# Expert results scaled at eviction and added into the residual by accumulating gathers in two passes

## The chip, the cores and the metric

The kernel is written in Bass, engine by engine, for one core of a Trainium2 chip. The metric is the device time of one execution in microseconds; lower is better.

## What is computed

A decoder trunk of two layers on 1024 tokens of width 1024, in float32. Each layer is an RMSNorm, one input projection shared by four kinds of heads, an output projection, a residual add, an RMSNorm and a mixture of experts, again with a residual add. The kernel ends with a norm. Only the end of the mixture of experts matters here:

```python
e_w = jax.nn.softmax(e_top, axis=-1) * g_p            # weights of a token's two experts
...
def expert_block(args):
    xb, e = args
    return (jax.nn.silu(xb @ w_gate[e]) * (xb @ w_up[e])) @ w_down[e]

ys = lax.map(expert_block, (xs, block_e)).reshape(n_slots, d)
return jax.ops.segment_sum(ys * slot_w[:, None].astype(ys.dtype), slot_tok, num_segments=t)
```

There are 32 experts with 256 hidden columns; each token goes to 2 of them, so 2048 rows are computed per layer, 64 per expert on average.

## The kernel before

**Data.** `X` (`residual`) holds the residual in SBUF: 128 partitions x 8 tiles of 128 tokens x 1024. `HT` (`normed_cols`) holds normed rows turned into columns, `YT` (`heads_cols`) the heads' results, `WR` (`w_ring`) weights. During the expert stage `WR` and `HT` hold gate and up weights of four experts (`Wgu`), `YT` their down weights (`Wd`), and most else lies in `G` (`group_arena`). In DRAM, `h2_dram` (`h_rows`) has the normed rows of all tokens and `ys_dram` (`expert_rows`) the experts' results, by slot: a slot is a row of a block of 128 rows, and there are 39 blocks and one more.

**Units.** VectorE ranks the experts by how many rows they have and gives every assignment of a token a slot (`dest_i`, two per token). The 16 experts with most rows are singles, with a block each; the other 16 go in pairs, 64 rows of a block for each. A block is a unit, so there are 24, ordered in eight "quads" of three: single, single, pair. Rows over an expert's share go to overflow units behind them, in a loop that a counter read from SBUF ends. Blocks 0 to 15 are the singles, 16 to 23 the pairs; quad q has the singles 2q and 2q + 1 and the pair 16 + q.

**The unit.** GpSimd gathers its rows of `h2_dram` into `xg` (an indirect DMA, line 747). TensorE turns them (L1238, L1244), ScalarE and VectorE take a half each (L1679, L2336), TensorE multiplies with gate and up (`gate_up`, L1259), ScalarE takes the silu (L1683), VectorE multiplies (L2340), TensorE turns (L1267), VectorE takes that (L2344), TensorE multiplies with down (`down`, L1280), and ScalarE and VectorE copy a half of the result each into `yb` (`take_y`, L1688, L2349). SyncE stores it to `ys_dram` (`store_y`, L645). TensorE's program is staggered: unit u's `gate_up`, then the turns of unit u - 1's hidden rows and of unit u + 1's inputs, then unit u - 1's `down`. VectorE and ScalarE follow in that order. Weights are loaded by SyncE in its program order: gate and up of the next quad (L620, L621) behind the end of this quad's `gate_up`, down (L624) behind the end of `down`. GpSimd issues all 24 row gathers, each as soon as its buffer is free.

**Start of the stage.** Behind the slot indices (`idx_i`, L2315) VectorE works out the overflow counter and the tokens' weights `wts` (L2318 to L2332), then takes its half of the first unit's rows. TensorE runs matmuls without use until the first rows are there (L1214).

**End of the stage.** SyncE, ScalarE, VectorE and TensorE pass the overflow loop; TensorE, ScalarE and VectorE meet in a barrier. GpSimd waits for all stores and issues 16 gathers of 512 KB, two per tile, from `ys_dram` into buffers `back`:

```python
for k in range(2):
    pool.indirect_dma_start(
        out=back[t][k], out_offset=None, in_=ys_dram,
        in_offset=bass.IndirectOffsetOnAxis(ap=dest_i[:, k, t:t + 1], axis=0)
    ).then_inc(back_in[t], 16)
```

VectorE combines tile by tile (`combine`, L2385): X += back0 * w0, X += back1 * w1. Then follows the norm of a tile: ScalarE squares and sums (L1359), VectorE scales the sum (L1777), ScalarE takes the root (L1361), VectorE inverts it (L1780) and writes the normed rows (L1781). TensorE turns them (L791, `turn_normed`), and ScalarE alone copies both halves (`take_whole_tile`, L1353). VectorE combines tile t + 1 before it norms tile t. At the kernel's start the norm of x has the same form without a combine, and there ScalarE and VectorE take a turned half each (`take_tile`: L1353, L1770).

**Into the next layer.** In layer 0 TensorE computes the next layer's first products behind the turns: behind tile 4's turn the first, which uses tiles 0 to 3, and one more behind each of tiles 5, 6 and 7 (`next_use`, L805). Their weights, chunks 0 and 1 of the input projection (1 MB and 2 MB), are loaded by SyncE into `WR` (`load_first`, L534) when all results are stored. In the last layer there is no product; SyncE stores each normed tile to the output (L683).

## Time and profile before

| | us |
|---|---|
| median of 3 runs | 2563.99 |
| lowest and highest | 2562.85, 2568.65 |
| the profiled execution | 2559.61 |
| its span (first to last instruction) | 2557.8 |
| TensorE busy | 2312.9 (90%) |
| VectorE busy | 1205.5 (47%) |
| ScalarE busy | 896.1 (35%) |
| GpSimd busy | 176.9 (7%) |

All times of rows are microseconds from the start of the span. Busy shares are means over stages with different limits: TensorE's 90% says little of the tails behind the two expert stages, of some 40 us each, where it mostly waits. The granted clock of TensorE is 1.00 at its full level, 2.4 GHz, and 0.50 at the lower, 1.2 GHz. "To landing" is the time from a DMA's issue to its semaphore. A gather's row names the tile that it fills: `group_arena` or `heads_cols` for the results, since `back` lies there.

### The profile page before, as it was taken

How to read it: one execution, taken by the hardware profiler on the slowest of the kernel's cores; microseconds unless marked ns; L12 is line 12 of the kernel's file. 1: busy time of each engine (PE TensorE's matmuls, PEld its weight loads, DVE VectorE, ACT ScalarE, POOL GpSimd, SP SyncE). 2: the span in 40 equal slices, each digit the busy share in tenths (PEclk: the TensorE clock that was granted, in tenths of full speed). 3: DMA queues.
4: the chain of work that ended last, by engine and by line, in shares of the span. 5: the costliest groups of instructions: out<-in, count | busy, mean ns of one | idle time of the engine just before them, and what ended most of it. 6: DMA issues, size and time to landing. Idle time of an engine off the chain costs nothing.

```text
span 2557.8 us, 29586 instructions
## 1 busy us (share of the span) xinstructions
PE 2312.9 (90%) x10142; PEld 1285.4 (50%) x10142; DVE 1205.5 (47%) x2666; ACT 896.1 (35%) x1842; POOL 176.9 (7%) x355
## 2 busy tenths in 40 slices
PE   5999989788999999999589998997989999899993
PEld 3476434555665554444246654445656655444442
DVE  4435288876663341111333445788766623311115
ACT  2122278864552111111222313797645511111113
POOL 0000032000000000000200000410000000000002
PEclk9999999899999989999799999998999999899996
DMA  6110001220100059999710001014010010799995
GB/s 255 28 52 27 33 14 43 80 63 1 50 1 28 33 216 371 422 423 422 297 43 30 33 27 37 14 52 129 2 50 1 1 36 33 302 408 422 422 414 214
DMA packets 101106, 353.79 MB, mean 138 GB/s; under 512 B 20246, under 2 KB 39660, under 8 KB 76396
## 3 DMA queue, kind: packets, MB, share of 16 engines
q1 hardware_dynamic: 89456, 310.15, 31.2%
q0 software_dynamic: 11520, 41.95, 4.3%
q8 instruction: 77, 1.26, 0.2%
q14 instruction: 53, 0.43, 0.1%
HBM read 296.03 MB, written 55.91 MB: 138 GB/s over the span
## 4 chain that ended last, share of the span: by engine, by line
PE 62%; DVE 13%; issue 8%; DMA 8%; ACT 6%; POOL 1%; SPq 1%; PEldq 1%; PEld 1%; DVEq 0%; ACTq 0%; POOLq 0%
PE bank L802 10%; PE bank L1259 9%; PE bank L1152 9%; DMA w_ring<-in_expert_w_up 7%; PE bank L882 6%; PE bank L791 6%; PE bank L805 5%; PE bank L1280 4%; PE bank L914 4%; ACT group_arena L1540 3%; DVE group_arena L2006 2%; DVE residual L2385 1%; PE bank L1169 1%; PE bank L1214 1%; DVE group_arena L1781 1%
## 5 line engine op out<-in xcount | busy, mean ns | idle before, releaser
L802 PE MATMUL bank<-w_ring,normed_cols 128*128 128x260 f32 (+4 forms) x1280 | 436.9, 494 | 10.7 <-ACT heads_cols L1565 8.9
L802 PEld LDWEIGHTS bank<-w_ring,normed_cols 128*128 128x128 f32 x1280 | 239.4, 193 | 180.1 <-issue 153.4
L805 PE MATMUL bank<-normed_cols,w_ring 128*128 128x512 f32 x640 | 281.1, 599 | 7.1 <-ACT group_arena L1442 6.2
L791 PE MATMUL bank<-ident,group_arena 128*128 128x128 f32 (+1 forms) x1200 | 183.4, 295 | 113.6 <-DVE group_arena L1781 91.2
L1259 PE MATMUL bank<-w_ring,group_arena 128*128 128x512 f32 x512 | 227.5, 597 | 7.5 <-DMA w_ring<-in_expert_w_up 4.0
L1152 PE MATMUL bank<-w_ring,heads_cols 128*128 128x512 f32 x512 | 225.5, 595 | 2.0 <-DVEq L261 2.0
L791 PEld LDWEIGHTS bank<-ident,group_arena 128*128 128x128 f32 (+1 forms) x1200 | 146.7, 150 | 158.3 <-issue 80.4
L805 PEld LDWEIGHTS bank<-normed_cols,w_ring 128*128 128x128 f32 x640 | 122.0, 193 | 158.7 <-issue 150.8
L882 PE MATMUL bank<-group_arena 96*128 96x512 f32 (+7 forms) x384 | 155.8, 510 | 25.1 <-ACTq L1430 13.1
L1280 PE MATMUL bank<-heads_cols,group_arena 128*64 128x512 f32 (+1 forms) x512 | 173.8, 596 | 2.8 <-DVE group_arena L2344 2.8
L2344 DVE COPY group_arena<-bank 128x256 f32<-128x256 f32 x48 | 20.3, 424 | 320.9 <-PE bank L1267 320.9
L1856 DVE TENSOR_REDUCE softmax_stats<-bank 128x1 f32<-128x768 f32 (+6 forms) x144 | 136.2, 946 | 62.1 <-PE bank L887 42.9
L1259 PEld LDWEIGHTS bank<-w_ring,group_arena 128*128 128x128 f32 x512 | 95.3, 190 | 135.9 <-issue 123.2
L1152 PEld LDWEIGHTS bank<-w_ring,heads_cols 128*128 128x128 f32 x512 | 95.3, 191 | 111.2 <-issue 108.9
L1540 ACT ACTIVATE group_arena<-heads_cols,group_arena 128x896 bf16<-128x896 f32 (+1 forms) x124 | 135.8, 1095 | 35.8 <-DVEq L2068 21.3
L2026 DVE TENSOR_SCALAR_CACHE_REDUCE group_arena<-group_arena 128x512 bf16<-128x512 f32 (+3 forms) x200 | 141.6, 754 | 11.5 <-DVE group_arena L2067 10.3
L747 POOL DMA_INDIRECT group_arena<-h_rows,group_arena x48 | 45.4, 945 | 1376.1 <-DVEq L2316 935.4
L1683 ACT ACTIVATE group_arena<-bank 128x256 f32<-128x256 f32 x48 | 18.4, 383 | 325.8 <-PE bank L1259 325.8
L1259 PE MATMUL bank<-normed_cols,group_arena 128*64 128x512 f32 x512 | 113.4, 595 | 11.1 <-DMA normed_cols<-in_expert_w_up 11.1
L1353 ACT ACTIVATE group_arena<-bank 128x512 f32<-128x512 f32 (+1 forms) x108 | 63.6, 589 | 141.7 <-PE bank L791 140.7
L2006 DVE SCALAR_TENSOR_TENSOR group_arena<-heads_cols,group_arena 128x512 f32<-128x512 f32 (+3 forms) x140 | 92.2, 658 | 25.3 <-ACT heads_cols L1531 18.6
L1770 DVE COPY group_arena<-bank 128x512 f32<-128x512 f32 (+4 forms) x124 | 69.3, 559 | 71.1 <-PE bank L791 68.6
(351 smaller groups left out, 3024.7 us busy)
## 6 DMA issues: line engine op xcount, KB each, us to landing
heads_cols<-in_expert_w_down SPq DMA_DIRECT2D x64, 1024.0 KB, 13.3
w_ring<-in_expert_w_gate SPq DMA_DIRECT2D x32, 1024.0 KB, 17.0
w_ring<-in_expert_w_up SPq DMA_DIRECT2D x32, 1024.0 KB, 19.1
normed_cols<-in_expert_w_gate SPq DMA_DIRECT2D x32, 1024.0 KB, 14.7
normed_cols<-in_expert_w_up SPq DMA_DIRECT2D x32, 1024.0 KB, 16.7
expert_rows<-group_arena SPq DMA_DIRECT2D x48, 512.0 KB, 13.5
w_ring<-in_w_in SPq DMA_DIRECT2D x6, 2048.0 KB, 9.0
expert_rows<-heads_cols SPq DMA_DIRECT2D x1, 8192.0 KB, 27.7
```

What stands on the lines that cost most here:

```text
L791: last = pe.transpose(bank(4 + r % 2)[0:rows, col:col + src.shape[0]], src, ident[0:src.shape[0], 0:src.shape[0]])
L802: m = pe.matmul(out[:, 0:width], HT[:, k, part * P:(part + 1) * P], w, start=(k == 0), stop=(k == K - 1))
L805: m = pe.matmul(out[0:width, :], w, HT[:, k, part * HALF:(part + 1) * HALF], start=(k == 0), stop=(k == K - 1))
L882: m = pe.matmul(L[:, c0:c1], a["q"](h, t), a["k"](h, c0, c1), start=True, stop=not (by_choice or diagonal))
L914: pe.matmul(O[i * HD:(i + 1) * HD, pair * P:(pair + 1) * P], KINDS[kind]["v"](h, b), pT[:, u % 2, at:at + P], start=(b == 0), stop=(b == t))
L1152: m = pe.matmul(bank(n % 4)[:, :], YT[:, k, t * P:(t + 1) * P], WR[:, (OUT_CHUNK + c) % 2, k, :], start=(k == 0), stop=(k == K - 1))
L1259: m = pe.matmul(gu_bank(s)[rows, :], xgT[:, s, k, rows], Wgu[w][:, :, k, :], start=(k == 0), stop=(k == K - 1))
L1280: m = pe.matmul(bank(6 + h)[rows, :], aT[:, s, k, rows], Wd[w][:, k, h * HALF:(h + 1) * HALF], start=(k == 0), stop=(k == 1))
L1540: act.activation(sign_junk[:, 0:w], flipped[t], ACT.Sign, bias=trial_bias[:, t - 2:t - 1], scale=SIGN_SCALE, accum_out=thr[:, 0, t - 2:t - ...
L1856: dve.tensor_reduce(stats(tile, heads[0], m, 1), src, AX_X, ALU.max, negate=True).then_inc(max_ready, 1)
L2006: ins = dve.scalar_tensor_tensor(s, rel[:, i, at:at + w], wI[:, t, j:j + 1], s, ALU.mult, ALU.add)
L2026: chain.go(dve.tensor_scalar(to, src(t), limit(t), 0.0, ALU.is_ge, ALU.add, accum_out=thr[:, 0, t - 2:t - 1]))
```

## The change

**Weights at eviction.** The two copies of a unit's result now multiply each row by its slot's weight: `take_y` gets `scale`, a column of `slot_w` (128 rows x 40 blocks). `slot_w` is made in unit 0: VectorE splits `wts` into three bfloat16 parts that add up to it, and builds masks; TensorE sums their products in 16 matmuls of 120 columns (`weights_to_slots`) between unit 1's turns and unit 1's `gate_up`; VectorE adds the parts (`spread_weights`). VectorE's `take_x(0, 0)` stands ahead of all this. The quad loops of ScalarE and VectorE are unrolled, since the weight's column differs by unit.

**Results added by DMA.** `back`, `combine` and `back_used` are gone. GpSimd gathers rows of `ys_dram` straight into `X` with addition, in two passes of 16. In the first the indices of late slots (blocks 14, 15, and 23 and up) are raised by 2^20, past the bound, so that their rows are skipped; in the second all others are. The first pass begins when the units of quad 6 are stored and all weights have landed; the second when all units are stored. Every gather waits until the one before it on the same tile has landed.

**Order elsewhere.** `load_first` of chunk c now comes ahead of the last three stores, behind the `gate_up` of units 21 and 22; overflow units use weight buffer 2 instead of 0. At the start, two more regions of `ys_dram` are zeroed (3 more blocks). Behind the barrier ScalarE waits for `back_in[t]` and squares; VectorE and ScalarE take a turned half each.

```diff
+        TURN_ORDER = [(0, 0), (1, 0), (2, 0)] + [at for t in range(T) for at in ((t, 1), (t + 3, 0)) if at[0] < T]
...
             sp.wait_ge(setup_zero, 1)
-            sp.dma_start(ys_dram[UNITS * P:, :].rearrange("(a p) d -> p a d", p=P),
-                         YT[:, 0:1, :].to_broadcast([P, SLOT_ROWS - UNITS, D])).then_inc(setup_dma2, 16)
+            for a, b in ((SINGLES - QUAD_SINGLES, SINGLES), (UNITS - 1, SLOT_ROWS)):
+                sp.dma_start(ys_dram[a * P:b * P, :].rearrange("(a p) d -> p a d", p=P),
+                             YT[:, 0:1, :].to_broadcast([P, b - a, D])).then_inc(setup_dma2, 16)
...
+                for c in range(2):
+                    sp.wait_ge(gu_done, UNITS - QUAD_UNITS + c + 1)
+                    with sp.If(l < DEPTH - 1):
+                        load_first(nc.s_assert_within(l + 1, 1, DEPTH - 1,
...
                 for i in range(QUAD_UNITS):
                     store_y(UNITS - QUAD_UNITS + i, unit_block(QUADS - 1, i), i)
...
+                def add_rows(t, k, at_i, n):
+
+                    wait_later(pool, back_in[t], 16 * n)
+                    pool.indirect_dma_start(
+                        out=X[:, t, :], out_offset=None, in_=ys_dram,
+                        in_offset=bass.IndirectOffsetOnAxis(ap=at_i[:, k, t:t + 1], axis=0),
+                        bounds_check=SLOT_ROWS * P - 1, oob_is_err=False, compute_op=ALU.add).then_inc(back_in[t], 16)
+
                 pool.wait_ge(idx_ready, 2)
+                for s in range(QUAD_UNITS):
+                    pool.wait_ge(y_out[s], 16 * (QUADS - 1))
+                for w in range(NW):
+                    pool.wait_ge(dn_in[w], 16 * QUADS)
+                for t, k in TURN_ORDER:
+                    add_rows(t, k, early_i, k)
+                pool.wait_ge(slot_weights, 1)
...
                 for s in range(QUAD_UNITS):
                     pool.wait_ge(y_out[s], 16 * QUADS)
+                for t, k in TURN_ORDER:
+                    add_rows(t, k, late_i, 2 + k)
                 for t in range(T):
...
-                    pool.wait_ge(back_in[t], 32)
+                    pool.wait_ge(back_in[t], 64)
...
-                    act.activation(yb[:, s, 0:HALF], bank(6), ACT.Copy).then_inc(y_lo, 1)
+                    act.activation(yb[:, s, 0:HALF], bank(6), ACT.Copy, scale=scale).then_inc(y_lo, 1)
...
-                        act.wait_ge(back_used, t + 1)
+                        act.wait_ge(back_in[t], 64)
                         norm_tile(t, T + t + 1)
                     if t >= 1:
-                        take_whole_tile(t - 1)
+                        take_tile(t - 1)
...
+                chain(dve.tensor_copy(w_parts[:, 0, :, :], wts[:, :, :]))
+                chain(dve.tensor_tensor(w_rest, wts[:, :, :], w_parts[:, 0, :, :], ALU.subtract))
+                chain(dve.tensor_copy(w_parts[:, 1, :, :], w_rest))
+                chain(dve.tensor_tensor(w_parts[:, 2, :, :], w_rest, w_parts[:, 1, :, :], ALU.subtract))
+                for k in range(2):
+                    chain(dve.tensor_tensor(blk_one, blk_of_slot, slot_at[:, 1:2, k * T:(k + 1) * T].to_broadcast([P, SLOT_ROWS, T]),
+                                            ALU.is_equal))
+                    chain(dve.tensor_tensor(w_hot[:, k, :, :, :], blk_one.unsqueeze(1).to_broadcast([P, 3, SLOT_ROWS, T]),
+                                            w_parts[:, :, k, :].unsqueeze(2).to_broadcast([P, 3, SLOT_ROWS, T]), ALU.mult))
+                chain(dve.tensor_copy(row_hot_w, row_hot))
+                dve.sem_inc(v2p, 1)
...
-                    dve.tensor_copy(yb[:, s, HALF:], bank(7)).then_inc(y_hi, 1)
+                    dve.tensor_scalar(yb[:, s, HALF:], bank(7), scale, None, ALU.mult).then_inc(y_hi, 1)
...
-                combine(0)
-                for t in range(T):
-                    if t + 1 < T:
-                        combine(t + 1)
-                    norm_tile(t, 4 * T + t + 1, T + t + 1)
+                for t in range(T + 1):
+                    if t < T:
+                        norm_tile(t, 4 * T + t + 1, T + t + 1)
+                    if t >= 1:
+                        take_tile(t - 1)
```

The order of a pass, as (tile, which of its two gathers), is (0,0) (1,0) (2,0) (0,1) (3,0) (1,1) (4,0) (2,1) (5,0) (3,1) (6,0) (4,1) (7,0) (5,1) (6,1) (7,1). The eight small operations that make the two index tables (`early_i`, `late_i`) stand on VectorE behind the copy of `row_hot_w`, ahead of unit 0's product.

## Rows read from the trace of the kernel before

**Rows 1.** The page: GB/s that the DMA engines moved, in 40 equal slices.
```profile
GB/s 255 28 52 27 33 14 43 80 63 1 50 1 28 33 216 371 422 423 422 297 43 30 33 27 37 14 52 129 2 50 1 1 36 33 302 408 422 422 414 214
```

**Rows 2.** Windows: us, then busy us and instructions by engine, TensorE's clock, DMA share, GB/s.
```profile
45.00:60.00 15.00, 15.00 (x48) 7.56 (x47) 2.73 (x5) 1.95 (x5) 0.00 (x0) 1.00 0.00 1
970.00:975.00 5.00, 5.00 (x21) 2.87 (x20) 1.44 (x3) 0.98 (x2) 0.94 (x1) 1.00 0.39 129
1230.00:1235.00 5.00, 5.00 (x26) 1.73 (x24) 0.43 (x1) 0.34 (x1) 0.00 (x0) 1.00 0.75 308
1235.00:1240.00 5.00, 4.48 (x17) 1.74 (x13) 0.75 (x2) 0.38 (x1) 0.00 (x0) 1.00 0.01 5
1265.00:1270.00 5.00, 1.94 (x8) 1.57 (x8) 4.46 (x6) 1.61 (x6) 4.09 (x4) 0.50 1.03 399
2490.00:2495.00 5.00, 5.00 (x26) 1.58 (x22) 0.00 (x0) 0.00 (x0) 0.00 (x0) 1.00 0.54 220
```

**Rows 3.** The chain of waits, layer 0: start us, us, what.
```profile
1246.95 2.62 DMA expert_rows<-group_arena
```

**Rows 4.** The timeline, layer 0's last unit and tail: start us, us, engine, line, operation.
```profile
1246.19 0.69 DVE L2349 COPY group_arena<-bank 128x512 f32<-128x512 f32 x1 [3.76 <-PE bank L1280]
...
1250.41 0.94 POOL L769 DMA_INDIRECT group_arena<-expert_rows,group_arena  x1 [60.23 <-DMA expert_rows<-group_arena]
1251.65 0.94 POOL L769 DMA_INDIRECT heads_cols<-expert_rows,group_arena  x1 [0.30 <-issue]
...
1256.87 1.28 DVE L2385 SCALAR_TENSOR_TENSOR residual<-group_arena,residual 128x1024 f32<-128x1024 f32 x1 [9.99 <-DMA heads_cols<-expert_rows,group_arena]
...
1284.25 1.97 PE L791 MATMUL bank<-ident,group_arena 128*128 128x128 f32 x8 [2.66 <-DVE group_arena L1781]
```

**Rows 5.** The timeline, last layer's tail.
```profile
2515.55 1.28 DVE L2385 SCALAR_TENSOR_TENSOR residual<-group_arena,residual 128x1024 f32<-128x1024 f32 x1 [10.05 <-DMA heads_cols<-expert_rows,group_arena]
...
2552.80 1.28 DVE L1781 SCALAR_TENSOR_TENSOR group_arena<-residual,rstd,gain 128x1024 f32<-128x1024 f32 x1
```

**Rows 6.** The gathers of results (line 769): ns min/median/max; landing from issue.
```profile
L769 POOL DMA_INDIRECT group_arena<-expert_rows,group_arena x16: 933/938/1906, 1250.4 to 2529.6; - x16
...
DMA to landing us min/median/max: 4.2/7.5/12.9
```

**Rows 7.** The timeline, start of the kernel: first norms of x.
```profile
16.53 1.06 ACT L1359 ACTIVATE group_arena<-residual 128x1024 f32<-128x1024 f32 x1
...
31.67 1.28 DVE L1781 SCALAR_TENSOR_TENSOR group_arena<-residual,rstd,gain 128x1024 f32<-128x1024 f32 x1
...
33.70 1.94 PE L791 MATMUL bank<-ident,group_arena 128*128 128x128 f32 x8 [1.76 <-DVE normed_cols L1770]
...
38.09 1.28 DVE L1781 SCALAR_TENSOR_TENSOR group_arena<-residual,rstd,gain 128x1024 f32<-128x1024 f32 x1
```

**Rows 8.** The timeline, start of layer 0's expert stage.
```profile
942.73 0.69 DVE L2311 TENSOR_TENSOR group_arena<-group_arena 128x1024 f16<-128x1024 f16 x1
...
943.54 0.83 PE L1230 MATMUL bank<-group_arena 128*128 128x40 f16 x8 [1.19 <-DVEq L2313]
...
946.29 0.15 DVE L2318 TENSOR_SCALAR group_arena<-group_arena 128x1 f32<-128x1 f32 x1
...
949.51 0.17 DVE L2332 TENSOR_TENSOR group_arena<-group_arena 128x8 f32<-128x8 f32 x1
...
954.58 0.69 DVE L2336 COPY group_arena<-bank 128x512 f32<-128x512 f32 x1 [4.90 <-PE bank L1244]
...
964.18 7.10 PE L1259 MATMUL bank<-w_ring,group_arena 128*128 128x512 f32 x16 [0.83 <-ACT group_arena L1679]
```

**Rows 9.** DMA issues of the whole kernel: KB each, median us to landing.
```profile
expert_rows<-heads_cols SPq DMA_DIRECT2D x1, 8192.0 KB, 27.7
...
normed_cols<-forgetting_q_k SPq DMA_DIRECT2D x2, 2048.0 KB, 19.9
```

153 lines of the change are left out of this document (87 added, 66 removed).

## The prediction

> **What bounds the kernel now.** I read the views from the whole to the place. The page's row of DMA rates [rows 1] shows the two expert stages as the stretches near 420 GB/s. The windows [rows 2] then say when the transfers stop: the rate is full until 75% of the window 1230 to 1235, so until 1233.7 us, and the next window moves nothing. TensorE still has 12.5 us of its last units: its last result is evicted at 1246.19 [rows 4]. In the last layer the transfers stop at 2492.7 (54% of 2490 to 2495, rows 2). So behind each expert stage there is a hole of 12 us in the DMA engines, and it is there that the change puts work. After the last eviction comes the tail: the store of the last unit (2.62 us [rows 3]), GpSimd's first gather 0.84 us behind its landing, and VectorE's first combine at 1256.87 [rows 4]. From there VectorE sets the pace: two combines of 1.28 us and a norm per tile, 4.63 us a tile. What the tail is worth differs by layer. In layer 0, TensorE needs tile 4 before its first product of the next layer (turned at 1284.25 [rows 4]); from there its own products set the end. So only tile 4 counts, 27.4 us behind the first combine. In the last layer tile 7 counts: normed at 2554.08, 38.5 us behind the first combine at 2515.55 [rows 5], with only its store behind it.
>
> **What is removed.** 16 combines per layer, 32 x 1.28 = 41 us of VectorE work. The rest of a tile then has the form of the kernel's start: ScalarE squares, VectorE norms and both engines take the turned halves, which is what the new loops do. The start shows the pace [rows 7]: first square at 16.53, norms at 31.67 (tile 4) and 38.09 (tile 6), so 3.2 us a tile. From "tile 0 complete" to "tile 4 turned" it takes 33.70 - 16.53 = 17.2 us; to the end of the eighth norm 38.09 + 2.7 + 1.28 - 16.53 = 25.6 us, with the one table load and TensorE at its lower clock, as in the tail (granted clock 0.50, rows 2). Against the 27.4 and 38.5 us of today this gives back **10.2 us in layer 0 and 12.9 us in the last layer**, if tile 0 is complete at the time of today's first combine.
>
> **What is added, and when tile 0 is complete.** GpSimd now issues 16 accumulating gathers, then 16 more, in one fixed order. No tile is complete before the second pass reaches it, and the second pass begins only when the first is issued. An issue takes 0.94 us and 0.30 between [rows 4, 6], so the first pass takes at least 16 x 1.24 = 19.8 us, and it starts only when all weights have landed: 1233.7 + 0.8 (GpSimd's wake) + 1.6 (below) = 1236.1, and 2495.1. (7,1), the last of the first pass, waits for (7,0), the 13th.
>
> The unknown is the DMA time of one accumulating gather; no row shows one. The lower end is a plain copy: 512 KB at 420 GB/s [rows 1], 1.25 us. A gain below that has no reason. The upper end is the slowest large transfer, 2048 KB in 19.9 us [rows 9], or 5.0 us per 512 KB. I take 2.5 us: it is nearest to the plain row, but an addition needs two operands, the row from memory and the old residual, and I price the second read like the first. About a tenth of the rows is left to the second pass (my estimate: of 2048 rows over 32 experts, the two singles and the pair that are late hold near the mean of 64, the pair less), so 2.25 us. The Trainium skill ("Collectives: The Full Stack", section on the bandwidth ceiling) says that an addition in a DMA emits two read descriptors per chunk on one ring and that reduce-scatter therefore runs at half of all-gather, 32.35 against 62.28 GB/s; no row here shows it. By that rule the sum stays as below, and by the plain row alone it is the first rival.
>
> Landing of the 13th, last layer: 2495.1 + 0.94 + 13 x 2.25 + two stores in between (2.5) + 2.0 (what a landing takes beyond issue and transfer: 4.2 - 0.94 - 1.25 [rows 6]) = 2529.8. The last three land 6.75 later, at 2536.6. The second pass moves little, but stands behind them: (0,0) at about 2536.8, (0,1) waits for it and lands 3.2 later: tile 0 is complete at 2540.0. The last norm ends 25.6 later, at 2565.6: **+11.5 us** against 2554.1.
>
> Layer 0 has the same and two things more in the queue: the store of unit 21 (1.25) and the next layer's first weights, which the change moves ahead of the last stores: 3 MB, 7.5 us at 420 GB/s. SyncE's queue is not held by that wait: the unit that it waits for is done before the store behind it can be issued. But the transfer fills the hole. So the 13th lands at 1236.1 + 0.94 + 29.25 + 2.5 + 8.75 + 2.0 = 1279.5, the last at 1286.3, tile 0 is complete at 1289.7, tile 4 is turned at 1306.9: **+22.6 us** against 1284.25. Moving the load gains nothing: those 7.5 us end today long before tile 4 is turned at 1284.25.
>
> **The start of the expert stage.** VectorE's weight work moves behind its first copy of turned rows, which ends at 955.27 [rows 8]. Moved: the 3.4 us from 946.29 to 949.68. New: four small operations (0.8), the masks (two of 320 and two of 960 elements; 1024 two-byte elements take 0.69: 2.1), a copy of 2048 (1.35), eight small ones (1.6). End 964.5; with the product (0.41) and the next copy (0.69) behind it the second unit's matmuls start at 965.75 instead of 964.18 [rows 8]: **+1.6 us a layer**, already in the sums. Bounds -0.6 (faster copies; nothing gained below the 0.83 us that TensorE waits now) and +2.8 (masks at four-byte pace). It isn't absorbed: TensorE is the bound there, and the DMA share falls to 0.39 in 970 to 975 [rows 2], so the loads shift too. The 16 small matmuls are covered by that wait (8 take 0.83 [rows 8]); without it they would cost 1.7.
>
> **Costed at nothing.** The scale in the evictions: one operation takes another's place, 0.69 us [rows 4], hidden by TensorE but for the last unit's. The 1.5 MB more of zeros at the start: the first fill takes 27.7 us [rows 9] and the DMA engines are idle from 45 to 60 [rows 2]; uncovered it would be 3.7 us. The unrolled loops: no engine but TensorE is near its limit there. The last store under load: it lands before the first pass has been issued. Overflow units don't run: the first gather of the tail waits for nothing but the last store [rows 4].
>
> Sum: 22.6 + 11.5 = 34.1 us. The profiled execution took 2559.6 us (span 2557.8), 4.4 under the median of 2564.0, against which I set the forecast: **2598 us**.
>
> **Rivals.**
> 1. *The addition is free, 1.25 us a gather (1.12 with a tenth missing).* For it: TensorE's hole is filled, and memory reads are what the copy rate measures. Against: the second operand. With the queue as above the 13th lands at 2515.1 and 1264.9, and tile 0 is complete at 2523.3 and 1273.0: -5.2 and +6.0, about 2565, no change. If the next layer's weights don't stand in the way (they may have landed by then), GpSimd's pace alone decides: the second pass starts at 1255.9 and 2514.9, tile 0 is complete 6.9 later, -4.2 and -6.7: 2553, **faster**. The mechanism decides at tile 0 complete by 1267 and 2528; that is at a gather of about 1.4 us. Chance 0.35, of it 0.24 for faster, 0.11 for no change.
> 2. *Skipped rows cost as much as moved ones* (the passes don't do what they say). Both passes then move 16 x 2.5 us. Last layer: tile 7 is complete 40 us behind 2540.6, and its norm ends at 2583.7, +29.6; layer 0: tile 4 is complete at 1320.3, turned at 1324, +40. About 2634. Against: the skipped index is outside the table. Chance 0.06.
> 3. *The addition runs at the slow row's pace, 5.0 us.* 16 gathers x 2.25 more in each layer: 2670. Against: that transfer fills 64 partitions only, a gather all 128. Chance 0.03.
>
> **How the numbers follow.** Forecast 0.56 (with it everything between 1.6 and 2.8 us a gather: 2580 to 2616). A measurement of this kernel can tell 0.2%, 5 us, from no change. Faster 0.24, same 0.12 (rival 1 with its queue), slower 0.64. The range reaches from rival 1's fast end, 2552, to the forecast's slow end, 2616; about 0.05 lies below and 0.09 above.
>
> **What would show it.** Landing of the accumulating gathers: at 2.5 us each the first pass's issues stall behind landings and (7,1) is issued near 2530; at copy pace near 2515. The DMA share should stay near 1.0 from 2493 to 2536. First square of the tail at 2540 (forecast), 2523 (rival 1), and the norms 3.2 us apart; in layer 0 tile 4 turned at 1307, 1290 or 1280. The second unit's matmuls 1.6 us later. In the second pass, landings of about 3.2 us speak against rival 2. The forecast is wrong if the first pass is issued 20 us after its start: then the addition costs no DMA time and the tail is shorter.

## The result, and the profile after

The changed kernel takes **2632.1 us** (median of 4 runs, 2626.5 to 2635.1), where the kernel before took 2565.6 us on the same chip: a ratio of **1.0241, interval 1.0223 to 1.0259**, 66.5 us more. The direction was forecast; the size was not: 34 us were forecast, and the range ended at 2616. The profiled execution took 2626.5 us (span 2624.7), 66.9 more than that of before.

First, where the 66.9 us lie. Two executions differ by some us before the expert stage of layer 0, where of the change only the zeros at the start have run: its slot indices are ready at 945.94 before and at 949.98 after (in the runs further down between 945.7 and 955.4). Here TensorE was granted a clock of 0.86 in 600 to 660, where the execution of before has 1.00. So from here on distances are taken from the moment at which VectorE has written the slot indices of a layer (DVE's only copy of 128x40 to int32: 945.94 and 2204.79 before, 949.98 and 2242.47 after). By these, +4.0 us lie ahead of the change, +33.6 from layer 0's indices to the last layer's, +29.2 behind those.

The page's row of DMA rates answers to [rows 1], the windows to [rows 2]:

```profile
GB/s 272 45 33 27 32 15 49 125 6 49 1 1 35 32 290 405 423 422 417 150 15 37 33 27 36 17 55 118 2 49 1 11 32 92 321 423 422 423 332 140
```

```profile
1240.00:1245.00 5.00, 4.48 (x20) 1.59 (x17) 0.75 (x2) 0.38 (x1) 2.65 (x2) 1.00 1.07 383
1265.00:1270.00 5.00, 0.00 (x0) 0.00 (x0) 0.00 (x0) 0.00 (x0) 3.69 (x3) 0.50 1.07 211
1300.00:1305.00 5.00, 0.80 (x4) 0.83 (x5) 1.62 (x4) 3.70 (x6) 4.37 (x3) 0.50 0.24 33
2535.00:2540.00 5.00, 4.49 (x17) 1.80 (x14) 0.75 (x2) 0.38 (x1) 3.38 (x3) 1.00 0.35 49
2555.00:2560.00 5.00, 0.00 (x0) 0.00 (x0) 0.00 (x0) 0.00 (x0) 3.10 (x2) 0.50 1.06 209
```

In layer 0 the hole is filled, as forecast: its start, 1235 to 1240 before with a share of 0.01, is 1240 to 1245 now (all is some 6 us later by then), with a share of 1.07. In the last layer its start is filled by a third (0.35). But behind the first gathers a full share moves only 209 to 211 GB/s, half of the 420 of a copy. And there is a second hole that did not exist before: from 1290 to 1315 the share is 0.11 to 0.24 while GpSimd goes on issuing. That is the second pass.

The gathers' line (771 now) answers to [rows 6]; "issue" is idle time in which GpSimd waited for nothing that the profile shows:

```profile
L771 POOL DMA_INDIRECT residual<-expert_rows,group_arena x64: 1537/1548/2542, 1242.0 to 2612.3; - x64
...
  issue: 70.5, 42
...
  ACT group_arena L1399: 111.0, 13
...
DMA to landing us min/median/max: 3.5/5.8/12.7
```

An issue takes 1.55 us, not the 0.94 of before. ScalarE waited 111 us for landings, of it 92 us for tile 0 in the two layers. The timeline of layer 0's tail, answering to [rows 4] (gathers; ScalarE's squares of tiles 0, 1 and 4; tile 4's turn and the first product):

```profile
1242.05 1.60 POOL L771 DMA_INDIRECT residual<-expert_rows,group_arena  x1 [45.48 <-issue]
...
1282.54 1.55 POOL L771 DMA_INDIRECT residual<-expert_rows,group_arena  x1 [2.51 <-DMA residual<-expert_rows,group_arena]
1290.75 1.55 POOL L771 DMA_INDIRECT residual<-expert_rows,group_arena  x1 [6.67 <-issue]
...
1296.31 1.55 POOL L771 DMA_INDIRECT residual<-expert_rows,group_arena  x1 [0.30 <-DMA residual<-expert_rows,group_arena]
...
1305.83 2.54 POOL L771 DMA_INDIRECT residual<-expert_rows,group_arena  x1 [0.30 <-DMA residual<-expert_rows,group_arena]
...
1321.32 1.55 POOL L771 DMA_INDIRECT residual<-expert_rows,group_arena  x1 [0.30 <-DMA residual<-expert_rows,group_arena]
...
1299.92 1.06 ACT L1399 ACTIVATE group_arena<-residual 128x1024 f32<-128x1024 f32 x1 [46.60 <-DMA residual<-expert_rows,group_arena]
...
1303.80 1.06 ACT L1399 ACTIVATE group_arena<-residual 128x1024 f32<-128x1024 f32 x1 [1.22 <-DMA residual<-expert_rows,group_arena]
...
1316.45 1.06 ACT L1399 ACTIVATE group_arena<-residual 128x1024 f32<-128x1024 f32 x1 [1.93 <-DMA residual<-expert_rows,group_arena]
...
1319.65 1.97 PE L819 MATMUL bank<-ident,group_arena 128*128 128x128 f32 x8 [2.07 <-DVE group_arena L1815]
1321.41 8.70 PE L833 MATMUL bank<-normed_cols,w_ring 128*128 128x512 f32 x16
```

Read it from the top. The first pass is issued from 1242.05 to 1284.1, and most of its issues wait for nothing but the issue before. Then comes a **gap of 6.67 us before 1290.75, put down to "issue"**. Then 16 more issues, most at 1.85 us each, two at 2.8, to 1322.9. The five squares from 1299.92 to 1316.45 come 4.1 us apart, each when its tile's last gather has landed. Tile 4 is turned at 1319.65, 369.7 us behind the slot indices; before it was 1284.25 - 945.94 = 338.3.

The last layer, answering to [rows 5]:

```profile
2536.01 1.60 POOL L771 DMA_INDIRECT residual<-expert_rows,group_arena  x1 [45.47 <-DMA expert_rows<-group_arena]
...
2575.24 1.55 POOL L771 DMA_INDIRECT residual<-expert_rows,group_arena  x1 [3.13 <-DMA residual<-expert_rows,group_arena]
2583.25 1.55 POOL L771 DMA_INDIRECT residual<-expert_rows,group_arena  x1 [6.46 <-issue]
...
2612.32 1.55 POOL L771 DMA_INDIRECT residual<-expert_rows,group_arena  x1 [0.30 <-issue]
...
2619.57 1.28 DVE L1815 SCALAR_TENSOR_TENSOR group_arena<-residual,rstd,gain 128x1024 f32<-128x1024 f32 x1
```

The same: 40 us of first pass, a gap of 6.46 us, 30.6 us of second pass, and the last norm ends 378.4 us behind the slot indices instead of 349.3.

The start of layer 0's expert stage, answering to [rows 8]:

```profile
959.22 7.11 PE L1287 MATMUL bank<-w_ring,group_arena 128*128 128x512 f32 x16 [0.83 <-ACT group_arena L1713]
...
967.05 3.66 PE L1317 MATMUL bank<-group_arena 128*128 128x120 bf16 x16
970.53 4.90 PE L1287 MATMUL bank<-w_ring,group_arena 128*128 128x512 f32 x11
...
963.38 0.66 DVE L2392 TENSOR_TENSOR group_arena<-group_arena 128x960 bf16<-128x960 bf16 x1
...
967.98 0.68 DVE L2354 COPY group_arena<-bank 128x512 f32<-128x512 f32 x1
```

VectorE is done with the weights at 967.6 and with its next copy at 968.7, but TensorE's 16 small matmuls end later, at 970.5. From the first unit's matmuls to the second's it is 11.31 us, 8.81 before, in both layers.

### The profile page after: what moved, and what is told of

It is laid out like the page before. It is cut to its first block, busy times and chain, and to the rows that moved or that the text cites. A ratio compares the mean times of both kernels' runs of the same rounds, so it can differ in the third digit from the quotient of the medians.

```text
span 2624.7 us, 29623 instructions
## 1 busy us (share of the span) xinstructions
PE 2327.5 (89%) x10174; PEld 1290.3 (49%) x10174; DVE 1187.8 (45%) x2690; ACT 893.8 (34%) x1826; POOL 244.3 (9%) x387
## 3 DMA queue, kind: packets, MB, share of 16 engines
q1 hardware_dynamic: 89856, 311.72, 30.6%
## 4 chain that ended last, share of the span: by engine, by line
PE 59%; DMA 11%; DVE 10%; issue 9%; ACT 6%; POOL 2%; SPq 1%; PEldq 1%; PEld 1%; POOLq 0%; DVEq 0%; ACTq 0%
PE bank L830 10%; PE bank L1180 8%; PE bank L1287 8%; DMA w_ring<-in_expert_w_up 7%; PE bank L910 6%; PE bank L819 5%; PE bank L833 5%; PE bank L942 4%; PE bank L1308 3%; DMA residual<-expert_rows,group_arena 3%; ACT group_arena L1574 3%; DVE group_arena L2040 2%; DMA expert_rows<-group_arena 1%; PE bank L1197 1%; POOL residual L771 1%
## 5 line engine op out<-in xcount | busy, mean ns | idle before, releaser
L910 PE MATMUL bank<-group_arena 96*128 96x512 f32 (+7 forms) x384 | 162.6, 529 | 24.5 <-ACTq L1464 12.5
L1399 ACT ACTIVATE group_arena<-residual 128x1024 f32<-128x1024 f32 x40 | 42.2, 1055 | 245.9 <-DVE residual L2281 134.8
L771 POOL DMA_INDIRECT residual<-expert_rows,group_arena x64 | 103.2, 1612 | 146.4 <-issue 70.5
## 6 DMA issues: line engine op xcount, KB each, us to landing
heads_cols<-in_expert_w_down SPq DMA_DIRECT2D x64, 1024.0 KB, 13.5
w_ring<-in_expert_w_gate SPq DMA_DIRECT2D x32, 1024.0 KB, 17.2
```

What stands on the lines that cost most here:

```text
L771: pool.indirect_dma_start(out=X[:, t, :], out_offset=None, in_=ys_dram, in_offset=bass.IndirectOffsetOnAxis(ap=at_i[:, k, t:t + 1], axis=0 ...
L910: m = pe.matmul(L[:, c0:c1], a["q"](h, t), a["k"](h, c0, c1), start=True, stop=not (by_choice or diagonal))
```

## The experiments

Eleven kernels were run. Each is the changed kernel but for the edit shown, or one of the others but for that edit, where this is said. Two of them leave out part of the sum, so that their last layer works on other numbers: copy_not_add and no_second_pass. Ratios are against the kernel before, run on the same chip in between; the kernels were spread over several chips.

| kernel | median us | ratio to before (interval) | tile 4 turned, last norm ended: us behind the slot indices |
|---|---|---|---|
| before | 2565.6 to 2571.1 | 1 | 338.3, 349.3 |
| changed | 2632.1 | 1.0241 (1.0223 to 1.0259) | 369.7, 378.4 |
| guarded_loop | 2619.2 | 1.0198 (1.0167 to 1.0228) | 365.4, 372.2 |
| copy_not_add | 2581.9 | one run | 350.6, 358.7 |
| load_behind_stores | 2629.3 | 1.0238 (1.0208 to 1.0267) | 371.6, 378.5 |
| one_pass | 2595.7 | 1.0111 (1.0080 to 1.0142) | 346.2, 362.8 |
| no_second_pass | 2563.6 | 0.9981 (0.9969 to 0.9993) | 334.7, 347.0 |
| scaled_only | 2574.6 | 1.0025 (1.0012 to 1.0037) | 340.4, 352.4 |
| half_by_dma | 2575.7 | 1.0022 (1.0009 to 1.0035) | 338.7, 354.8 |
| stores_last | 2576.2 | 1.0024 (1.0011 to 1.0038) | 337.8, 349.1 |
| weights_in_a_row | 2581.4 | 1.0047 (1.0032 to 1.0062) | 345.7, 356.2 |
| by_layer | 2579.7 | 1.0038 (1.0023 to 1.0053) | 343.6, 356.5 |
| by_layer_strided | 2570.5 | 0.9998 (0.9987 to 1.0009) | 338.5, 352.9 |

### The gap between the passes: guarded_loop

```diff
+                with pool.If(n_over > 0):
-                with pool.Fori(0, OVER) as j:
-                    with pool.If(n_over > j):
+                    with pool.Fori(0, OVER) as j:
+                        with pool.If(n_over > j):
...
```

> The loop over the 15 possible overflow units on GpSimd's side is entered only if there are overflow units; nothing else differs from the changed kernel. Theory: the 6.67 us (layer 0) and 6.46 us (last layer) between the last gather of the first pass and the first of the second are GpSimd going through 15 empty iterations. Then both gaps fall to under 1.5 us, the second pass and all that follows it come 5.5 to 6.5 us earlier in each layer, and the kernel takes 11 to 13 us less: 2619 to 2621 us. Rival: the gap is a wait for something that is late there (the landing of the last unit's store, or a transfer in the queue in front of it). Then the gaps stay at over 5 us and the time stays within 3 us of 2632.

Measured: 2619.2 us. GpSimd's timeline at the same place:

```profile
1289.56 1.55 POOL L771 DMA_INDIRECT residual<-expert_rows,group_arena  x1 [2.50 <-DMA residual<-expert_rows,group_arena]
1291.41 1.55 POOL L771 DMA_INDIRECT residual<-expert_rows,group_arena  x1 [0.30 <-issue]
```

The gap is gone (0.30 us; in the last layer from 2573.00 to 2574.85 likewise). The ratio falls from 1.0241 to 1.0198, some 11 us (4.3 us at tile 4 and 6.2 us at the last norm). The gap was GpSimd going through 15 iterations with nothing in them, 0.42 us each. The kernel before has the same loop at the same place, but there GpSimd was waiting 60 us anyway [rows 4]; the change put work ahead of it and behind it. The Trainium skill ("Advanced Engine Details and Errata", section on control flow timing) gives 51 ns for a branch and 108 ns for a comparison with one; an iteration here takes more than twice their sum, so the loop holds more than these two steps.

### The price of the addition: copy_not_add

```diff
-                        bounds_check=SLOT_ROWS * P - 1, oob_is_err=False, compute_op=ALU.add).then_inc(back_in[t], 16)
+                        bounds_check=SLOT_ROWS * P - 1, oob_is_err=False).then_inc(back_in[t], 16)
```

> All 32 gathers of a layer write their rows instead of adding them; rows out of bounds are skipped as before. The residual is overwritten by the expert results and their sum is left out, so that the second layer computes on other numbers. It prices the addition by itself. Theory: an added row costs two reads' worth of DMA time; without the addition the DMA engines move 420 GB/s instead of 210 in the stretch of the first pass, and the first pass, which then has 1.25 us of transfer per gather, is bound by GpSimd's issues. Whether an issue takes 1.55 us (as in the changed kernel) or 0.94 us (as a plain gather before) is open. If 1.55 goes with the bounds, the first pass takes 16 x 1.85 = 30 us from first to last issue instead of 40 us and the kernel some 15 to 22 us less in all (2610 to 2617); if it goes with the addition, 16 x 1.24 = 20 us, the second pass too is 10 us shorter, and the kernel takes some 40 us less (about 2590). Rival: 210 GB/s is a limit of the indirect write with bounds, not of the addition; then the first pass stays at 40 us and the time within 5 us of 2632.

Measured: 2581.9 us in a single run, 50 less than with the addition; 2590 or 2610 to 2617 were expected. At the two places of the table it is 19.1 and 19.7 us, 39 in all; the rest lies outside the tails, so that the addition is priced at 39 us rather than 50. Its gathers, and the window of its first pass in the last layer:

```profile
L771 POOL DMA_INDIRECT residual<-expert_rows,group_arena x64: 987/993/1570, 1241.6 to 2568.3; - x64
...
DMA to landing us min/median/max: 2.5/4.3/8.7
```

```profile
2525.00:2530.00 5.00, 0.00 (x0) 0.00 (x0) 0.00 (x0) 0.00 (x0) 2.37 (x3) 0.86 0.97 355
```

The addition has two prices, and both count. In transfer: 355 GB/s at a share of 0.97 without it, 210 with it. And on GpSimd: 0.99 us for an issue with bounds and without addition, 1.55 with both; the version one_pass, below, has the addition without bounds and takes 1.545; a plain gather takes 0.94 [rows 6]. So bounds cost 0.05 us beside a plain gather and nothing beside an addition, and the **addition 0.56 us an issue** beside bounds, in 64 issues 36 us of GpSimd. The first pass goes from 40.5 to 27.4 us (layer 0), from first to last issue, and the second from 30.6 to 20.7. The gap in front of the second pass stays (7.2 us in layer 0, from 1270.0 to 1277.2), as it should.

### The next layer's first weights: load_behind_stores

```diff
-                for c in range(2):
-                    sp.wait_ge(gu_done, UNITS - QUAD_UNITS + c + 1)
-                    with sp.If(l < DEPTH - 1):
-                        load_first(...)
...
                 for s in range(QUAD_UNITS):
                     sp.wait_ge(y_out[s], 16 * QUADS)
+                for c in range(2):
+                    with sp.If(l < DEPTH - 1):
+                        load_first(...)
```

> The load of the next layer's first weights (3 MB, layer 0 alone) goes back behind the wait for all of the layer's stores, as in the kernel before. Theory, as in the prediction: the load takes 7.5 us of the DMA engines in the hole in which the first pass runs, so without it the first pass in layer 0 is issued up to 7.5 us sooner (40.5 us from first to last issue becomes 33 to 36) and the kernel takes 4 to 7.5 us less. The load then falls into the second pass, where the DMA share is 0.2 to 0.28, and has to have landed before the next layer's first products at about 1320, which it does. Rival: the load slips in beside the gathers or is done before they fill the queue; the first pass of layer 0 (40.5 us) is as long as that of the last layer (39.2 us), which has no such load, and that speaks for it. Then the time changes by under 2 us, and the load only moves to where it delays the gathers of the second pass.

Measured: no difference (1.0238 against 1.0241). Of the rival the time holds; but the load delays gathers of the first pass, not of the second. Its windows in layer 0:

```profile
1265.00:1270.00 5.00, 0.00 (x0) 0.00 (x0) 0.00 (x0) 0.00 (x0) 3.07 (x3) 0.50 1.07 222
...
1285.00:1290.00 5.00, 0.00 (x0) 0.00 (x0) 0.00 (x0) 0.00 (x0) 1.55 (x1) 0.50 1.05 304
```

The load now arrives at 1264 to 1292 amid the gathers of the first pass (222 to 304 GB/s at a share of 1.05 to 1.07), which takes 42.3 us instead of 40.5. In the changed kernel it arrives right behind the last expert weights, while the first gathers are still being issued: 383 GB/s in 1240 to 1245, where the last layer, which has no such load, moves 49 GB/s in 2535 to 2540. Most of it costs nothing: from its first to its last issue the first pass takes 40.5 us in layer 0 and 39.2 in the last layer.

### One pass: one_pass

```diff
-                for s in range(QUAD_UNITS):
-                    pool.wait_ge(y_out[s], 16 * (QUADS - 1))
-                for w in range(NW):
-                    pool.wait_ge(dn_in[w], 16 * QUADS)
-                for t, k in TURN_ORDER:
-                    add_rows(t, k, early_i, k)
...
-                    add_rows(t, k, late_i, 2 + k)
+                    add_rows(t, k, dest_i, k)
```

(and `bounds_check` dropped, with waits for 32 where 64 stood)

> No first pass: 16 accumulating gathers per layer, without bounds, all behind the last store, each with the whole index. Scaled evictions, weights and everything else are as in the changed kernel. Theory: the second pass costs GpSimd's issues, 1.85 us each for almost no data, and the loop in front of it 6.5 us; a single pass costs 16 gathers of 2.5 us of transfer. Behind the last store (about 1256 and 2497 + 12 = 2509 as in the kernel before, + 4 us for the weights in each layer) tile 0 is complete after (0,0), (1,0), (2,0) and (0,1), about 12 us on, and each further tile 5 us later. So tile 4 is complete 32 us behind the store and tile 7 about 44 us; in the changed kernel it is 1320 - 1256 = 64 us for tile 4 turned, and the last norm at 2620, 105 us behind 2515. So I expect 2575 to 2595 us, 40 to 55 us less than the changed kernel: most of the loss is the second pass itself, not the addition. Rival: the addition at half the rate is what costs; then one pass behind the store loses what two passes lost, and it stays above 2610. If an issue takes 1.55 us here too, the addition lengthens it; if 0.94, the bounds do.

Measured: 2595.7 us, just above what was expected: 36 us less than two passes, 26 more than before. ScalarE's squares of tiles 2 and 3 in layer 0:

```profile
1284.13 1.06 ACT L1393 ACTIVATE group_arena<-residual 128x1024 f32<-128x1024 f32 x1 [2.84 <-DMA residual<-expert_rows,group_arena]
...
1289.12 1.06 ACT L1393 ACTIVATE group_arena<-residual 128x1024 f32<-128x1024 f32 x1 [2.88 <-DMA residual<-expert_rows,group_arena]
```

The tiles come 4.99 us apart: two added rows of 2.5 us each. So with a single pass DMA is the bound, and slower than VectorE's 4.63. In the last layer the last gathers are issued 4.7 to 7.1 us apart, and the last norm comes 13.5 us later than before, tile 4's turn in layer 0 only 7.9. That the stores of the output are the reason is shown below in another version (stores_last), not in this one.

### What a free second pass would be worth: no_second_pass

```diff
-                for t, k in TURN_ORDER:
-                    add_rows(t, k, late_i, 2 + k)
```

(on top of guarded_loop; ScalarE waits for `y_out` and for 32 instead of 64)

> The version with the guarded loop, without its second pass: the rows in the expert results of the last three units (about a tenth) are left out of the sum. ScalarE waits for the last store before its first square. It shows what the first pass costs when nothing comes behind it. Theory: the whole loss is the second pass, 16 issues of 1.85 us (30 us) for a tenth of the rows; the first pass lies mostly in the hole. Then tile 0 is complete when the last eviction is done, tiles follow the landings of the first pass, tile 7 is complete about 6 us behind the last issue, and the time is 2550 to 2567 us, 50 to 70 us less than with the guarded loop (2619) and no more than the kernel before (2570 on this chip). Rival: the first pass itself, at half rate and behind all weights, ends as late as the tail of the kernel before; then some 25 to 35 us less are left to gain by leaving out 30 us of issues in each layer only where they were last, and the time stays above 2580.

Measured: 2563.6 us, a ratio of 0.9981 (0.9969 to 0.9993). Tile 4's turn and the last norm:

```profile
1280.71 1.97 PE L818 MATMUL bank<-ident,group_arena 128*128 128x128 f32 x8 [2.15 <-DVE group_arena L1816]
...
2552.18 1.28 DVE L1816 SCALAR_TENSOR_TENSOR group_arena<-residual,rstd,gain 128x1024 f32<-128x1024 f32 x1
```

Against guarded_loop that is 55.6 us less, as the theory says: behind this first pass, it is the second that the kernel loses by. But the other half of the reading matters more. **With the second pass gone altogether the kernel is only 5 us faster than before** (3.6 us at tile 4, 2.3 at the last norm). The first pass, 40 us long, ends as late as the old tail; so the rival's first half holds too. As long as the first pass stays as it is, no way of making the second cheap can make this change worth much.

### The way of the weights: scaled_only

```diff
+                def bring_rows(t, k):
+                    out, how = back[t][k], {}
+                    pool.indirect_dma_start(
+                        out=out, out_offset=None, in_=ys_dram,
+                        in_offset=bass.IndirectOffsetOnAxis(ap=dest_i[:, k, t:t + 1], axis=0),
+                        **how).then_inc(back_in[t], 16)
...
+                    for k in range(2):
+                        chain(dve.tensor_tensor(X[:, t, :], back[t][k], X[:, t, :], ALU.add))
```

(the passes and their tables are gone; loops of the tail as before)

> The results are scaled at eviction (with the matmuls, the copies and the unrolled loops of the changed kernel, its zeros and its early load), but the tail is that of the kernel before: 16 plain gathers of 0.94 us behind the last store and two additions per tile on VectorE, now without a weight in them. No tables for two passes. It prices the way of the weights by itself. Theory: the 16 matmuls stand in TensorE's way with 3.66 us and take the place of a wait of 0.83 us, so the second unit starts 2.5 to 2.9 us later in each layer, nothing of it is won back, and the additions take 1.28 us as the combines did: 5 to 8 us more than before (2575 to 2578). Rival A: the delay is covered by what the units wait for anyway, then within 2 us of before. Rival B: the additions without a weight are quicker than 1.28 us; then each layer's tail is shorter by five or eight times twice the difference and the time may come out below 2570.

Measured: 2574.6 us, 1.0025 (1.0012 to 1.0037): 6 us more than before, as the theory has it. Start of layer 0's expert stage, and two additions of the tail:

```profile
972.30 3.68 PE L1314 MATMUL bank<-group_arena 128*128 128x120 bf16 x16
975.80 8.45 PE L1284 MATMUL bank<-w_ring,group_arena 128*128 128x512 f32 x16
...
1272.93 1.22 DVE L2440 TENSOR_TENSOR residual<-group_arena,residual 128x1024 f32<-128x1024 f32 x1 [0.35 <-DMA heads_cols<-expert_rows,group_arena]
1274.19 1.22 DVE L2440 TENSOR_TENSOR residual<-heads_cols,residual 128x1024 f32<-128x1024 f32 x1
```

The additions are a little cheaper without a weight (1.22 us instead of 1.28, the tiles 4.51 us apart instead of 4.63). The matmuls take 3.68 us, and the next 16 take 8.45 here, 8.74 in the last layer, where 7.05 to 7.10 is usual. The changed kernel shows 7.05 in layer 0 and 8.74 in the last layer. What goes with it is TensorE's granted clock. These are the windows of scaled_only in layer 0, of the changed kernel in layer 0 and of the changed kernel in the last layer:

```profile
975.00:980.00 5.00, 5.00 (x12) 2.47 (x11) 0.59 (x3) 0.00 (x0) 0.00 (x0) 0.66 1.00 416
970.00:975.00 5.00, 5.00 (x15) 2.45 (x14) 0.59 (x3) 0.00 (x0) 0.00 (x0) 1.00 0.99 409
2260.00:2265.00 5.00, 5.00 (x19) 3.01 (x18) 1.84 (x7) 0.07 (x1) 0.93 (x1) 0.84 1.02 428
```

So it is in all 20 stages whose masks are written in order (two of the changed kernel and two each of nine others): in the 9 in which the 16 matmuls take 7.05 us the granted clock over them is 1.00, in the 11 in which they take 8.4 to 8.7 us it is 0.76 to 0.80. The way of the weights thus costs 2.5 us by the small matmuls in every stage and 1.4 to 1.7 us more in some, by the clock. The first gather of the tail is issued 3.6 us (layer 0) and 4.2 us (last layer) later than before, counted from the slot indices, which is about the sum of the two.

### One row of two by DMA: half_by_dma

```diff
-                    out, how = back[t][k], {}
+                    out, how = (X[:, t, :], dict(compute_op=ALU.add)) if k == 0 else (back[t][1], {})
...
-                    for k in range(2):
-                        chain(dve.tensor_tensor(X[:, t, :], back[t][k], X[:, t, :], ALU.add))
+                    chain(dve.tensor_tensor(X[:, t, :], back[t][1], X[:, t, :], ALU.add))
```

(against scaled_only)

> One pass behind the last store: of each tile's two gathers the first adds into the residual by DMA, the second is a plain one, and VectorE adds it. 16 issues, no wait between them. A tile then costs 2.5 + 1.25 = 3.75 us of transfer, 1.85 + 1.24 = 3.1 us of GpSimd and 1.28 + 2.05 = 3.3 us of VectorE, where the kernel before takes 4.63 us of VectorE. Theory: 3.75 us a tile, so 0.9 x 5 = 4.4 us less to tile 4 in layer 0 and 0.9 x 8 = 7 us less in the last layer, minus 1 us in each for the first tile and 2.5 to 2.9 us in each for the weights: 3 to 5 us less than before (about 2566), and 8 to 12 less than the version with scaled evictions alone. Rival: gathers that add and gathers that copy get in each other's way in the queue, or a tile waits for the landing of both (6 and 10 us each in the version with one pass), and the tiles come 4.6 us apart or more: 2573 to 2580.

Measured: 2575.7 us, no less than scaled_only, where 8 to 12 us less had been expected (about 2566); it lies in the rival's 2573 to 2580. VectorE's additions of tiles, two in layer 0 and two in the last layer, and a window of each:

```profile
1282.50 1.23 DVE L2439 TENSOR_TENSOR residual<-heads_cols,residual 128x1024 f32<-128x1024 f32 x1 [0.40 <-DMA heads_cols<-expert_rows,group_arena]
...
1286.23 1.23 DVE L2439 TENSOR_TENSOR residual<-heads_cols,residual 128x1024 f32<-128x1024 f32 x1 [0.38 <-DMA heads_cols<-expert_rows,group_arena]
...
2552.72 1.23 DVE L2439 TENSOR_TENSOR residual<-heads_cols,residual 128x1024 f32<-128x1024 f32 x1 [1.67 <-DMA heads_cols<-expert_rows,group_arena]
...
2557.71 1.23 DVE L2439 TENSOR_TENSOR residual<-heads_cols,residual 128x1024 f32<-128x1024 f32 x1 [1.65 <-DMA heads_cols<-expert_rows,group_arena]
```

```profile
1280.00:1285.00 5.00, 2.38 (x10) 1.57 (x9) 3.59 (x7) 3.09 (x8) 4.39 (x3) 0.50 1.04 293
2550.00:2555.00 5.00, 1.97 (x8) 1.57 (x8) 2.82 (x5) 2.20 (x7) 0.00 (x0) 0.50 1.05 315
```

In layer 0 they come 3.73 us apart, as the sum of 2.5 and 1.25 says, and tile 4 is turned 1.7 us sooner than in scaled_only. In the last layer they come 5.0 us apart, and the last norm is 2.4 us later. The windows show the DMA engines full in both.

### Why 5.0 us in the last layer: stores_last

```diff
-                        sp.wait_ge(rows_normed, T + t + 1)
+                        sp.wait_ge(rows_normed, 2 * T if t == 0 else T + t + 1)
```

(against half_by_dma)

> The version that lets the DMA engines add one row of two, with one change: in the last layer the eight stores of the output wait until the last tile is normed. It asks why its tiles came 3.73 us apart in layer 0 but 5.0 us apart in the last layer from the fourth on. Theory: the last layer's tiles share the DMA engines with the output: 2.5 + 1.25 + 1.25 = 5.0 us. Without the stores between them the norms come 3.75 us apart to the end, the last one ends 5 to 6 us sooner behind the first addition (35.2 + 1.28 us today), and the stores (10 us) stand behind it, so that the kernel takes 2 to 5 us more in all. Rival: the gathers that add get slower for another reason (both of a tile go to one queue, the clock); then the tiles stay 5.0 us apart and the kernel takes 8 to 9 us more.

Measured: the same two additions of the last layer:

```profile
2553.67 1.23 DVE L2439 TENSOR_TENSOR residual<-heads_cols,residual 128x1024 f32<-128x1024 f32 x1 [0.36 <-DMA heads_cols<-expert_rows,group_arena]
...
2557.44 1.23 DVE L2439 TENSOR_TENSOR residual<-heads_cols,residual 128x1024 f32<-128x1024 f32 x1 [0.43 <-DMA heads_cols<-expert_rows,group_arena]
```

3.77 us apart, and the last norm ends 349.1 us behind the slot indices instead of 354.8. So the stores of the output (1.25 us of transfer a tile) were what made 3.75 into 5.0: in the last layer the added rows compete with the output. The stores then stand behind the last norm, and the total is the same within its interval (1.0024 against 1.0022); the 2 to 5 us more that were expected can't be told from this.

### Columns side by side: weights_in_a_row

```diff
-        w_hot = g(2592, ...).rearrange("p (k i n t) -> p k i n t", k=2, i=3, n=SLOT_ROWS)
+        w_hot = g(2592, ...).rearrange("p (k t i n) -> p k i n t", k=2, i=3, n=SLOT_ROWS)
```

(against scaled_only)

> The version with scaled evictions alone, with one change: the 120 columns that each of the 16 small matmuls of the weights reads lie side by side in memory instead of every eighth element. It asks why these 16 took 3.66 us, 0.23 each, where the 8 of the row indices (40 columns, every eighth element too) took 0.83 us, 0.10 each. Theory: the step from column to column costs; side by side they take about 0.10 each, 1.7 us in all, the second unit starts 2 us sooner in each layer and the kernel takes 4 us less than with scaled evictions alone: about 2570. VectorE's masks then write in steps and may take longer; its work ends 3 us ahead of TensorE's today. Rival: the number of columns costs, 120 against 40; then they stay at 3.4 to 3.7 us and the time within 1 us.

Measured: 2581.4 us, 1.0047: slower, where 4 us less were expected. TensorE, then one of VectorE's two masks:

```profile
974.43 1.82 PE L1314 MATMUL bank<-group_arena 128*128 128x120 bf16 x16 [5.98 <-DVEq L2398]
976.04 9.28 PE L1284 MATMUL bank<-w_ring,group_arena 128*128 128x512 f32 x16
...
964.62 4.35 DVE L2395 TENSOR_TENSOR group_arena<-group_arena 128x960 bf16<-128x960 bf16 x1
```

The theory of the matmuls holds: 16 take 1.82 us instead of 3.68, so the step between columns cost half of their time. The next 16 take 9.28 us in layer 0 and 8.46 in the last layer, at a granted clock of 0.69 and 0.80. What was taken for harmless was not: VectorE writes each mask of 960 two-byte elements in 4.35 us instead of 0.66, and TensorE waits 5.98 us for it. The Trainium skill ("Advanced Engine Details and Errata", section on VectorE's performance modes) asks for a unit step in the innermost dimension for the fast mode that it lists for an operation on two tensors, two elements a cycle. The trace agrees in direction; the factor here is 6.6, more than that mode alone gives.

### The best of the parts: by_layer and by_layer_strided

```diff
+                with dve.If(l < DEPTH - 1):
+                    tail((1,))
...
+                with dve.If(l > DEPTH - 2):
+                    tail((0, 1))
```

(GpSimd branches likewise: `compute_op=ALU.add` for k == 0 only ahead of the last layer; by_layer has the columns side by side, by_layer_strided every eighth element)

> The best that I can put together of the parts: scaled evictions with the columns of the weights side by side; in layer 0 the DMA engines add one row of two, in the last layer both are gathered plainly and VectorE adds them without a weight (4.51 us a tile instead of 4.63). Theory: of the 3.6 us that the weights cost in a layer 1.6 are left; layer 0 gains 1.7 us by the DMA's addition and 0.5 in the first tile against the version with scaled evictions alone, the last layer 0.9 by the cheaper additions: within 3 us of the kernel before (2566 to 2571). Rival: the matmuls stay at 3.66 us; then 2572 to 2574. If it were 10 us faster than before, an addition by DMA would be worth more than these rows say.

> As the best version put together before, with the weights' columns every eighth element again: side by side they took TensorE 1.82 us instead of 3.68, but VectorE 4.35 and 4.22 us instead of 0.66 for each mask, so that TensorE waited 6 us for them. Theory: against the version by layer with the columns side by side (2579.7, where the kernel before took 2571.1) each layer gets back about 3 us of that wait, some 6 us in all, and the time is 2571 to 2575, 0 to 4 us above the kernel before: what the DMA's addition gives in layer 0 and the cheaper additions in the last layer (1.7 + 0.9 us) pays for less than half of what the weights cost. Rival: below 2566, then the parts add up to a gain after all.

Measured: 2579.7 us for by_layer, where 2566 to 2571 were expected, or 2572 to 2574 by the rival; it has the slow masks of weights_in_a_row. by_layer_strided takes 2570.5 us where before takes 2569.6, a ratio of **0.9998 (0.9987 to 1.0009): no change**. In layer 0 tile 4 is turned 338.5 us behind the slot indices (before 338.3), in the last layer the last norm ends 352.9 behind them (349.3). What the parts give just about pays for the way of the weights. No version with scaled evictions that sums all rows beats the kernel before.

## Why the prediction was wrong, step by step

The prediction failed at a step that it costed at nothing, GpSimd's empty loop between the two passes, and at the price of GpSimd's issues. The steps of the last layer add up like this, counted from the slot indices, forecast against measured: first gather 290.3 against 293.5 (+3.2); from there to the end of the wait for the 13th gather 34.7 against 39.2 (+4.5); from there to tile 0 complete 10.2 against 17.4 (+7.2); to the last norm's end 25.6 against 28.2 (+2.6). With the forecast's +11.5 that is +29.0, where +29.1 is measured. In layer 0: first gather +1.9, first pass -2.9, tile 0 complete +7.2, tile 4 turned +2.5; with +22.6 that is +31.3, measured +31.4.

So the tails hold 60.5 us where 34.1 were forecast. The 26 us between are 14.4 at "tile 0 complete" (12.5 of them the empty loop), 5.1 in the tiles' pace behind it, 5.1 in the first gather and 1.6 in the first pass. The other 6 us of the 66.9 lie in stages that the change doesn't touch: 4.0 ahead of it and 2.3 between tile 4's turn and the last layer's indices, where guarded_loop and load_behind_stores take as long as the kernel before.

- **The loop between the passes: the step that failed most.** The forecast costed overflow units at nothing ("overflow units don't run"). True, but the 15 empty iterations are run, and the change took away their cover, the 60 us of waiting. 6.67 and 6.46 us in the trace, some 11 us in guarded_loop. For most terms costed at nothing the prediction names the work that hides them; for the loop, on the one engine whose queue the change filled, it named none and didn't ask what became of it.
- **The price of an issue, 0.94 us, taken from a plain gather.** With the addition it is 1.55 (copy_not_add, one_pass). By this reading it barely matters in the first pass, where transfers of 2.25 us exceed 1.85 us of issue. It decides the second: the forecast let it run at 16 x 1.24 = 19.8 us, faster than the tiles' own 3.2 us; it takes 30.6 us, and two issues per tile (3.7 to 4.6 us) set the tiles' pace in layer 0. The terms "17.2 us to tile 4 turned" and "25.6 us to the eighth norm" became 19.7 and 28.2 by it.
- **Half rate for an added row: right.** 210 GB/s at a full share, so 2.5 us for 512 KB. The Trainium skill's reason ("Collectives: The Full Stack", section on the bandwidth ceiling), two reads for each chunk, agrees with the factor of two; the trace shows the rate, not the reads. The first pass came out 4.5 us longer in the last layer. I put most of that down to its start, where the first gathers leave the engines partly idle (49 GB/s in 2535 to 2540); no run separates it.
- **The first weights of the next layer at 7.5 us: mis-sized.** 1.3 us is left of it (40.5 against 39.2), since it fills just that idle start. load_behind_stores shows it from the other side. That the load gains nothing either was right.
- **The weights at +1.6 us a layer: mis-sized, and for the wrong reason.** VectorE's chain was even 0.9 us shorter than forecast (it ends at 967.6, and 4.0 of that are this run's own, where 964.5 was forecast). But the 16 matmuls, held to be covered by TensorE's wait and worth 1.7 us uncovered, take 3.66 and end after it: 2.5 us in each layer. In the last layer the lower clock adds 1.7 us more (8.74 against 7.05 us), a term that the prediction doesn't have. The prediction had taken the price of 8 matmuls with 40 columns for those with 120; half of the 3.66 us is the step between columns. scaled_only prices the whole way at 6 us, with 13 cheaper tiles already set against it.
- **Rival 1, the addition for free,** is out by the 210 GB/s, and copy_not_add puts 39 us on it in the tails. **Rival 2, skipped rows cost as much as moved ones,** had nearly the right total (2634) by the wrong mechanism: the second pass of layer 0 moves 13 to 33 GB/s, its landings have a median near 4 us, and what lasts is GpSimd's issues, 1.55 us each as in the first pass. **Rival 3** is out by the same 210 GB/s.
- **The range.** Its ends don't come out of the sum: by the sum's own terms 1.6 and 2.8 us a gather give 2572 and 2607, not 2580 and 2616. The measured time lies above either.
- The zeros, the unrolled loops, the scale in the evictions (0.69 us became 0.75) and the last store show nothing, as forecast.

The whole, by experiments: scaled evictions 0.25% (6 us), additions by DMA in one pass instead of by VectorE another 0.86% (22 us), a second pass in place of one another 1.3% (33 us), of it a third the empty loop. These differences are between kernels measured on different chips, each against the kernel before. What was removed, 41 us of VectorE work, is real, but it paced a tail that a slower engine (DMA, 5.0 us a tile) and a slower queue (GpSimd, two issues of 1.85 us) then paced in its place.

**Open:** behind the small matmuls the granted clock falls in 11 of 20 stages and not in the other 9, although TensorE has run the same instructions before it, with no wait in between; the kernel before shows 1.00 and 7.10 us there in both layers. What decides it wasn't tried. Whether the first gathers' idle start could be filled wasn't tried either.

## What to carry to other kernels

Before splitting work into an early and a late pass over the same list, price the pass and not the bytes: a gather whose rows are nearly all skipped costs its issue in full, and here that was 1.85 of the 2.5 us of a full one. A price taken from a plain operation does not hold for the one with an addition, on any of the engines it touches: measure transfer and issue apart. And when an engine that used to wait gets work, every empty loop, check and table in its queue between the two pieces comes out of hiding at full price; guard such loops as a whole, so that the usual case skips them once.

## What the runs showed of the hardware

- A gather that adds into on-chip memory moves 209 to 211 GB/s with the DMA share at 1.06 to 1.07; plain ones 399 [rows 2]. Two added rows a tile come 5.0 us apart, an added and a plain one 3.73, and with a store of 512 KB between them 5.0.
- GpSimd's issue of a gather with 128 rows: 0.94 us plain, 0.99 with bounds, 1.545 with addition, 1.55 with both. In the second pass single ones take up to 2.5. Rows left out by the bounds save transfer (13 to 33 GB/s) but nothing of the issue.
- 15 empty iterations of a loop with a condition in it: 6.4 us on GpSimd.
- 16 matmuls of 120 two-byte columns: 3.68 us with every eighth element, 1.82 side by side. VectorE's product of 960 two-byte elements: 0.66 us written in order, 4.35 written to steps of 120 elements.
- The same 16 matmuls of 128x512 take 7.05 us at a granted clock of 1.00 and 8.4 to 8.7 us where it is 0.76 to 0.80; which it is differs between stages that run the same instructions.
